# First stage of a three-part block: input and weights by turns on one queue, products among the transposes, angles later

## The reference, cut to what matters

```python
h_res = jnp.concatenate([meta, x], axis=1)
pos = jnp.concatenate([meta_pos, positions + N_META], axis=1)
for l in range(DEPTH):
    h = rmsnorm(h_res, norm_gain[l])
    proj = h @ w_in[l]
    u_pool, z_pool, c_q, c_kv, k_rope, z_mla, g_pool, g_mla = jnp.split(proj, IN_SPLIT_POINTS, axis=-1)
    ...
# in apply_rope
ang = pos.astype(jnp.float32)[..., None] * inv_freq
cos = jnp.cos(ang)[:, :, None, :]
sin = jnp.sin(ang)[:, :, None, :]
```

## Time and profile before

| what | value |
|---|---|
| median of three runs | 1821.43 us (1821.07 to 1821.55) |
| the profiled execution | 1820.53 us, its span 1818.7 us |
| TensorE, VectorE, ScalarE, GpSimd busy | 96%, 65%, 48%, 18% of the span |
| first product of the first layer | starts at 22.25 us |
| c3, the fourth latent chunk | starts at 43.08 us |

### The profile page before, as it was taken

One profiled execution on the slowest core, in us unless ns is written; L12 is line 12 of the kernel. 1 busy time (PEld: TensorE's weight loads), 2 busy tenths in 40 slices (PEclk: granted clock), 3 DMA queues, 4 the chain that ended last, 5 costly groups with the idle time before them and its releaser, 6 DMA issues.

```text
span 1818.7 us, 25325 instructions
## 1 busy us (share of the span) xinstructions
PE 1750.9 (96%) x10156; PEld 1441.4 (79%) x10156; DVE 1185.6 (65%) x1704; ACT 873.7 (48%) x1407; POOL 331.2 (18%) x222
## 2 busy tenths in 40 slices
PE   8999999999999999999999999999999979999993
PEld 7998788999897667788999766765578758888882
DVE  5566645554466655555775698577674467989896
ACT  5425434234334544334344455466552246777771
POOL 3323222001243223001000375300010010000001
PEclk8999999999999999999999999999999989999996
DMA  6203112223312202323222200213152269999994
GB/s 189 76 24 99 47 48 70 94 70 116 96 59 75 70 30 65 100 93 121 76 88 93 70 24 24 70 47 115 50 193 93 93 219 363 402 405 402 405 362 169
DMA packets 156095, 241.31 MB, mean 133 GB/s; under 512 B 9593, under 2 KB 101018, under 8 KB 155978
## 3 DMA queue, kind: packets, MB, share of 16 engines
q1 hardware_dynamic: 148602, 212.88, 33.9%
q0 software_dynamic: 4464, 16.25, 2.4%
q10 hardware_dynamic: 2912, 10.55, 1.4%
HBM read 223.41 MB, written 16.25 MB: 132 GB/s over the span
## 4 chain that ended last, share of the span: by engine, by line
PE 51%; DVE 5%; ACT 4%; issue 2%; DMA 1%; POOL 0%; POOLq 0%; ACTq 0%; DVEq 0%
PE acc L1377 15%; PE acc L876 10%; PE acc L1120 9%; PE acc L1145 7%; PE acc L1209 2%; PE acc L1223 2%; PE acc L1240 1%; PE acc L1363 1%; PE acc L1231 1%; PE acc L1105 1%; DVE upad L2702 1%; DVE qk L2702 1%; ACT v L1973 1%; DMA qk<-y_rows,back_rows 0%; PE acc L1027 0%
## 5 line engine op out<-in xcount | busy, mean ns | idle before, releaser
L876 PE MATMUL acc<-h_split,ring_split 128*128 128x264 f32 (+1 forms) x864 | 269.5, 312 | 0.0
L876 PEld LDWEIGHTS acc<-h_split,ring_split 128*128 128x128 f32 x864 | 162.3, 188 | 9.6
L1145 PE MATMUL acc<-ring_split,h_split 128*128 128x256 f32 x384 | 108.0, 281 | 0.0
L876 PE MATMUL acc<-h_split,qk_split 128*128 128x264 f32 (+1 forms) x288 | 92.7, 322 | 1.3 <-DVE ring_split L2206 1.3
L876 PE MATMUL acc<-ring_split,qk_split 128*128 128x264 f32 (+1 forms) x288 | 92.2, 320 | 0.0
L2206 DVE TENSOR_TENSOR ring_split<-ring,o_split 128x1024 fp32r<-128x1024 f32 (+1 forms) x32 | 44.8, 1417 | 64.2 <-ACT o_split L1535 64.1
L3140 POOL DMA_INDIRECT latent<-h_rows,rows_of x16 | 18.3, 1141 | 355.7 <-PE acc L1363 214.0
L2206 DVE TENSOR_TENSOR ring_split<-ring,qk_split 128x1024 fp32r<-128x1024 f32 (+1 forms) x56 | 59.4, 1069 | 34.0 <-ACT qk_split L1535 34.0
L876 PE MATMUL acc<-h_split,krope_split 128*128 128x264 f32 (+1 forms) x240 | 79.4, 331 | 1.9 <-POOL ring_split L3031 1.9
L3017 POOL TENSOR_TENSOR latent<-latent 128x528 f32<-128x528 f32 x18 | 26.9, 1492 | 293.0 <-ACT latent L1530 292.6
L1377 PE MATMUL acc<-qk_split,krope_split 128*128 128x512 f32 x264 | 78.1, 397 | 0.0
(11 more groups left out here) (596 smaller groups left out, 5536.5 us busy)
## 6 DMA issues: line engine op xcount, KB each, us to landing
ring<-in_w_in SPq DMA_DIRECT2D x64, 1024.0 KB, 5.3
ring<-in_w_expert_gate SPq DMA_DIRECT2D x10, 2048.0 KB, 12.8
ring<-in_w_expert_up SPq DMA_DIRECT2D x10, 2048.0 KB, 12.0
ring<-in_w_expert_down SPq DMA_DIRECT2D x10, 2048.0 KB, 13.4
ring<-in_w_out SPq DMA_DIRECT2D x12, 1024.0 KB, 5.2
y_rows<-gate ACTq DMA_DIRECT2D x16, 512.0 KB, 6.9
hres<-in_w_expert_up SPq DMA_DIRECT2D x3, 2048.0 KB, 11.6
qk<-in_w_expert_down SPq DMA_DIRECT2D x3, 2048.0 KB, 12.9
```

Of the source, the lines that this page charges most:

```text
L876: ins = nc.tensor.matmul(dst[0:rows_, half, 0:x.shape[1]], w[:, k, :], x, start=(k == 0 and i == 0), stop=(k == last and i == 2), skip_gro ...
L1145: ins = nc.tensor.matmul(dst[:, side, 0:WIDE], x[k][:, rows_], w, start=(k == 0 and part == 0), stop=(k == DC - 1 and part == 2), skip_gro ...
```

## The change

x is loaded in two halves of its columns (1 MB each) on SP's queue, by turns with the first two granules of weights; positions, the rest of the constants, the other two granules and all small loads come behind. Only the first layer's first gain, the identity and the meta tokens are loaded by ScalarE. The first gain is turned by itself (`first_gain`), the others later (`vecs`). TensorE runs three fillers at first, turns chunks 0 to 3 with some fillers among them, and turns chunk k + 4 behind step k of `first_products`, in the accumulators of chunks 2 and 3 (`accumulator_again`). VectorE makes the angles in four pieces, each behind the lower weights of one of the entries 3 to 6; ScalarE takes Sin and cos behind c6. The product `ss_h`, the tables and the root stand in the first layer behind c6 instead of c2 (`SUMS_AT`).

```diff
+        SUMS_AT = (6, 2)
...
-            load_first(0, 2)
+            for i in range(2):
+                sp.dma_start(xin[:, :, i * HID:(i + 1) * HID],
+                             a["x"][0, :, i * HID:(i + 1) * HID].rearrange("(j p) d -> p j d", p=P)).then_inc(x_loaded[i], 16)
+                load_first(i, i + 1)
+            sp.dma_start(angles[:, 0, META:T].bitcast(I32),
+                         a["positions"].to_broadcast([ROPE, SEQ])).then_inc(const_loaded, 16)
+            sp.dma_start(const[:, P:], a["const"][:, P:K_TIE]).then_inc(const_loaded, 16)
+            load_first(2, 4)
+            sp.wait_ge(pool_made, at(pool_made, "vrows"))
+            for l in range(LAYERS):
+                load_gains(l)
...
+            def accumulator_again(label, reader, back):
+
+                for x in jobs[-back]:
+                    released(*x)
+                slot = (len(jobs) - back) % ACCS
+                jobs[-back] = [(label, reader, n.layer)]
+                n.slots[label, n.layer] = slot
+                return acc[:, slot, :, :]
...
                         if k == DC - 1:
                             done(ins, ("c", c))
+                    if n.layer == 0 and k < 4:
+                        n.layer = None
+                        turn_input(k + 4)
+                        n.layer = 0
...
+            for c in range(4):
+                turn_input(c)
+                keep_busy(acc[:, 3, 1, 0:256], 1 if c < 2 else 0, work[:, 0, 0:256])
+            keep_busy(acc[:, 3, 1, :], 3, work[:, 0, 0:512])
+
             def turn_tables():
 
+                pe.wait_ge(const_loaded, 32)
+                pe.wait_ge(gains_loaded, at(gains_loaded, "gains"))
+                dst = accumulator("vecs", dve_evacuated)
+                done(nc.tensor.transpose(dst[:, 0, 0:LAYERS * LV], vrows[0:LAYERS * LV, :],
+                                         ident[0:LAYERS * LV, 0:LAYERS * LV]), "vecs")
...
-                    if c == 2:
+                    if c == SUMS_AT[n.layer]:
                         product("ss_h", act_evacuated, [ones[:, :]], lambda k: sum_sq,
                                 before=lambda k: pe.wait_ge(square_sum, at(square_sum, "sum", back=1)))
                         if n.layer == 0:
...
+            act.dma_start(first_gain[0:DC, :], a["norm_gain"][0].rearrange("(k m) -> k m", k=DC))\
+                .then_inc(first_gain_loaded, 16)
+            act.dma_start(const[:, 0:P], a["const"][:, 0:P]).then_inc(ident_loaded, 16)
+            act.dma_start(metain[0:META, :], a["meta_tokens"]).then_inc(meta_loaded, 16)
...
+            input_upper(0)
+            input_copy(2)
+            input_upper(1)
+            first_upper(0)
+            first_upper(1)
+            input_upper(2)
+            input_upper(3)
+            input_copy(5)
+            input_upper(4)
+            first_upper(2)
+            input_upper(5)
+            input_copy(7)
+            input_upper(6)
+            input_upper(7)
             for c in range(DC):
                 squares(c, ("x", c), ("sq0", c))
             for n.layer in range(LAYERS):
...
                     weights_upper(JOBS_A, c + 3)
-                    if c == 2:
+                    if c == SUMS_AT[n.layer]:
+                        if n.layer == 0:
+                            n.layer = None
+                            rotation_tables()
+                            n.layer = 0
                         root("ss_h", inv[:, :], D, 1)
...
+            input_copy(0)
+            input_copy(1)
+            input_lower(0)
+            input_lower(1)
+            first_lower(0)
+            first_lower(1)
+            input_copy(3)
+            input_lower(2)
+            input_lower(3)
+            input_copy(4)
+            input_lower(4)
+            input_copy(6)
+            first_lower(2)
+            for c in range(5, DC):
+                input_lower(c)
...
                 if n.layer == 0:
+                    for i in range(3, DC):
+                        weights_lower(JOBS_A, i)
+                        if i < 7:
+                            n.layer = None
+                            (angles_begun, angles_turns, angles_reduced, angles_ended)[i - 3]()
+                            n.layer = 0
                     n.layer = None
                     turned_tables()
                     n.layer = 0
+                    layer_vectors()
+                    inverse("ss_h", inv[:, :])
```

More of the change, by code:

```diff
@@ L276, in program @@
         vrows2 = qkf[:, 5 * D + P:5 * D + 2 * P]
+        first_gain = qkf[:, 5 * D + 2 * P:5 * D + 3 * P]
+        angles = v[:, :, :].rearrange("p c t -> p (c t)")[NOPE:QK, 0:2 * T].rearrange("p (a t) -> p a t", a=2)
         sum_sq = gate[:, 1, :]
@@ L393, in program @@
         const_loaded = sem("const_loaded")
-        x_loaded = sem("x_loaded")
+        x_loaded = [sem(f"x_loaded{i}") for i in range(2)]
+        meta_loaded = sem("meta_loaded")
+        ident_loaded = sem("ident_loaded")
+        first_gain_loaded = sem("first_gain_loaded")
         vec_loaded = sem("vec_loaded")
@@ L655, in _, with load_gains @@
         def _(sp):
[L656 to L662 removed]
+            def load_gains(l):
                 r = LV * l
@@ L916, in _, with turn_input @@
             done(ins, "meta")
-            for c in range(DC):
-                dst = accumulator(("x", c), act_evacuated if c in X_BY_ACT else dve_evacuated)
+            def turn_input(c):
+                if c % 4 == 0:
+                    pe.wait_ge(x_loaded[c // 4], 16)
+                by = act_evacuated if c in X_BY_ACT else dve_evacuated
+                if c < 4:
+                    dst = accumulator(("x", c), by)
+                else:
+                    dst = accumulator_again(("x", c), by, 4 - c % 2)
                 for i in range(4):
@@ L2184, in _ @@
-            big = 1.5 * 2 ** 23
-            chain(ts(turns, ang, 1.0 / (2 * math.pi), big, ALU.mult, ALU.add))
-            chain(ts(turns, turns, -big, None, ALU.add))
-            rest, parts = 2 * math.pi, []
-            for bits in (8, 12, 24):
-                e = 2.0 ** (bits - 1 - math.floor(math.log2(abs(rest))))
-                parts.append(math.trunc(rest * e) / e if bits < 24 else rest)
-                rest -= parts[-1]
-            for part in parts:
-                chain(stt(out=ang, in0=turns, scalar=-part, in1=ang, op0=ALU.mult, op1=ALU.add))
@@ L2194, in _, with angles_begun @@
[L2194 to L2201 removed]
+            def angles_begun():
+                dve.wait_ge(const_loaded, 32)
+                nc.vector.tensor_copy(ang[:, 0:META], const[NOPE:QK, K_META:K_META + META])
+                chain(nc.vector.tensor_copy(ang[:, META:T], angles[:, 0, META:T].bitcast(I32)))
+                chain(ts(ang[:, META:T], ang[:, META:T], float(META), None, ALU.add))
+                chain(ts(ang, ang, const[NOPE:QK, K_FREQ:K_FREQ + 1], None, ALU.mult))
@@ new lines, in angles_turns, with angles_reduced @@
+            def angles_turns():
+                big = 1.5 * 2 ** 23
+                chain(ts(turns, ang, 1.0 / (2 * math.pi), big, ALU.mult, ALU.add))
+                chain(ts(turns, turns, -big, None, ALU.add))
+            def angles_reduced():
+                rest, parts = 2 * math.pi, []
+                for bits in (8, 12, 24):
+                    e = 2.0 ** (bits - 1 - math.floor(math.log2(abs(rest))))
+                    parts.append(math.trunc(rest * e) / e if bits < 24 else rest)
+                    rest -= parts[-1]
+                for part in parts:
+                    chain(stt(out=ang, in0=turns, scalar=-part, in1=ang, op0=ALU.mult, op1=ALU.add))
@@ new lines, in angles_ended @@
+            def angles_ended():
+                chain(ts(angles[:, 0, :], ang, 3.1415925, -3.1415925, ALU.min, ALU.max))
+                dve.wait_ge(dve_step, now(dve_step))
+                made(stt(out=angles[:, 1, :], in0=angles[:, 0, :], scalar=-1.0,
+                         in1=angles[:, 0, :], op0=ALU.mult, op1=ALU.max), "angles")
+            result("first_gain")
+            slot = n.slot(("first_gain"))
+            evacuated(nc.vector.tensor_copy(vecs[:, 0:DC], acc[:, slot, 0, 0:DC]), "first_gain")
@@ L2285, in _ @@
                     n.layer = 0
-                for i in range(6, DC):
-                    weights_lower(JOBS_A, i)
+                    layer_vectors()
+                    inverse("ss_h", inv[:, :])
+                else:
+                    for i in range(2, 6):
+                        weights_lower(JOBS_A, i)
+                    inverse("ss_h", inv[:, :])
+                    for i in range(6, DC):
+                        weights_lower(JOBS_A, i)
                 def gain_of(x, count):
```

119 lines of the change are left out of this document (52 added, 67 removed).

## The result

The changed kernel takes 1827.62 us (median of seven runs, 1826.96 to 1829.36), the kernel before 1821.19 beside it: ratio 1.0036, 95% interval 1.0026 to 1.0046, so 6.4 us slower. The profiled execution took 1828.59 us, its span 1826.7 (before 1818.7). The busy line of the page says nothing of it: TensorE is busy 1754.5 us, 96% of the span as before.

A forecast was written before the change was run, and what follows sets the result against it. TensorE, busy 96% of the span, was taken to bound the kernel. The terms -5.5 + 6.9 + 3.2 = +4.6 us, added to the median of 1821.43, gave 1826.0 us, range 1820.5 to 1829.5.

The forecast's parts named there:

- Term 1: Start of chunk 3 on TensorE, still waiting for the sum of squares: 37.6 instead of 43.08 us, -5.5 us.
- Term 2: Tables moved behind chunk 6: chunk 7 waits for Sin, cos, two table loads and the root, +6.9 us.
- Rival 3: Between chunks 6 and 7: chunk 7 does not wait for the root, so faster, 1817.5 us; chance 0.06.
- rival 4: Loads at the start: halves and granules share the engines instead of landing by turns, 1829.0 us; chance 0.05.
- rival 5: ScalarE behind chunk 6: a table change holds it twice as long as its load, 1828.6 us; chance 0.03.
- Term 3: TensorE's clock falls to half behind the new waits before chunk 3 and around chunk 6: 1.6 us each, +3.2.
- Rival 1: TensorE's clock stays full through both new waits, before chunk 3 and around chunk 6: 1822.8 us; chance 0.22.
- Rival 2: At the start, the early products run at half clock, squares begin at 24.6 us: 1827.7 us; chance 0.16.
- Sum: Whole forecast shift, read at chunk 7's square: -5.5 + 6.9 + 3.2 = +4.6 us.
- the shift goes through to the end: Behind chunk 7: later stages keep their code, so the +4.6 us there was to reach the kernel's end.

The follow-up runs named there:

- the run with all mends: Changed kernel with small loads first, table load drawn forward, first sum of squares in its own buffer and behind c4, Sin and cos behind c5: 1809.54 us.

## Why the prediction was right, and where its sizes were off

Direction, place and range hold (1826.0 forecast, 1820.5 to 1829.5; 1827.6 measured). That the time came within 1.6 us of the forecast is luck in part: two errors, in term 1 and behind c7, offset each other. By its terms:

- **Term 1**, start of c3: -5.5 us forecast, -1.0 measured (42.08 for 43.08), outside its bounds of -9.2 to -3.0. The mechanism was as described: TensorE idle 4.73 us (5.0 forecast) for a chain of 14.58 us from first square to c3 (14.7 forecast). From the first product to the squares it took 10.0 us (10.1 forecast). What was mis-sized is the stretch ahead of the first product, so that the squares began at 27.50, not 22.9, and even later than the upper bound of 25.35. Two sentences failed. One is "Identity, first gain and meta tokens are 130 KB on the other queue and land before": small and issued early was taken for landing early. Putting them first brings 24.18, 3.3 us. The other is that ScalarE's first table load "now waits for the meta copy, 7.2 to 8.5": it waited for chunk 0's copy, which adds its 1.28 us to the path. With it drawn forward too the squares begin at 23.62, and at 23.10 in the run with all mends, 0.2 us from the forecast; executions of one start differ by more (27.50 to 28.35 in the six kernels that keep the changed start).
- **Term 2**, tables behind c6: +6.9 forecast, and c7 starts 6.69 us after c6's square (6.7 forecast), by the two waits named. Rival 3 (c7 does not wait for the root) is out, rival 4 (halves and granules do not come by turns) too, with x's halves at 5.8 and 12.2 us (6.3 and 12 forecast) and the first weights between them at 9.7, and so is rival 5: the root starts 0.02 us after its table load ends, as before. "0 to 0.3 us" for the lower weights behind the reciprocal was right for this kernel (they are done at 79.3, ahead of c7's end), but only because c7 is late.
- **Term 3**, the clock: +3.2 forecast, +4.4 measured, its upper bound: 1.5 behind c3 (42.08 to 49.72 is 7.64 us, 43.08 to 49.19 before is 6.11) and 2.9 behind c6 (15.58 - 5.80 - 6.9). Rival 1 is out. The row behind 22.25, from which the 1.6 us were taken, is not a clean case: the granted clock was 0.50 from 19 us on, ahead of the wait of 2.77 us.
- **Rival 2**, early products at half clock, did not come true as stated: the first products ran at full clock (1.00 from 17.5 to 19 us). What ran at 0.50 were the turned chunks and fillers ahead of them, from 8.4 to 15.1 us. With the small loads first these ran at 1.00, and from the meta tokens' transposes to the first product it took 8.2 us instead of 9.1, so this cost at most 0.9 us; it is contained in term 1.
- **Sum**: +10.3 at c7 against +4.6. That "the shift goes through to the end" failed as well: at the end of the profiled executions 8.0 us are left (spans of 1826.7 and 1818.7), in the medians 6.4, which brought the time near the forecast. The largest piece lies near 1030 us, in code that the change does not touch. Before:

```profile
1024.64 2.88 DVE L2654 SCALAR_TENSOR_TENSOR gate<-gate,rt 128x512 f32<-128x512 f32 x1
...
1024.61 2.36 POOL L3102 TENSOR_TENSOR ring_split<-ring,o_split 128x1024 fp32r<-128x1024 f32 x1 [152.08 <-ACT o_split L1535]
...
1038.01 0.49 DVE L2653 TENSOR_SCALAR gate<-gate,rt 128x512 f32<-128x512 f32 x1
```

With the change:

```profile
1034.39 0.75 DVE L2776 SCALAR_TENSOR_TENSOR gate<-gate,rt 128x512 f32<-128x512 f32 x1
...
1034.51 2.85 POOL L3224 TENSOR_TENSOR ring_split<-ring,o_split 128x1024 fp32r<-128x1024 f32 x1 [152.05 <-ACT o_split L1580]
...
1044.71 0.56 DVE L2775 TENSOR_SCALAR gate<-gate,rt 128x512 f32<-128x512 f32 x1
```

GpSimd begins 0.03 us before VectorE in the one, 0.12 after it in the other, and VectorE's instruction, for which TensorE waits, takes 2.88 or 0.75 us. From there to the last row, the next turn of the same work, it takes 13.4 us before and 10.3 with the change: 3.1 us of the shift are gone. The two runs made from the kernel before have GpSimd's 2.36 and the long turn as well, the eight made from the changed one 2.84 and the short turn. What shifts the two engines against each other by 0.15 us is open. Later about 1.3 us are lost again, around 1490 us, where the clock is at half for 13.7 us instead of 10.2. The last 1.6 us, between the profiled executions and the medians, are scatter between executions.

## What to carry to other kernels

An earlier start is worth little until the chain behind it is shortened too (here 4.7 us at the first product, 1.0 us at c3): before predicting a gain, follow each buffer that the early work writes to whoever still holds it, and see which slack was just enough. Where several waits lie behind each other, price the ones that are covered: in the kernel before, moving the sum behind c6 cost 6.4 us without Sin, because a reciprocal of 3.45 us stood ready to take its place. Here a pause of 4.7 us cost its length and then 1.5 us of slow clock behind it, and the mends were worth more together (18 us) than the sum of each alone (12.6).

## What the runs showed of the hardware

- Small loads on a second queue are not fast by being small: 64 KB took 5.4 and 6.6 us to land beside 1 MB loads on SP's queue, longer than the first of those (5.1); as SP's first issues they took 1.8 and 2.1 us and are there before TensorE asks for them at 5.93 us. Whether the queue or the order made the difference was not separated.
- VectorE and GpSimd slow each other: an instruction on 32x528 with one tensor as its input takes 1.45 us while GpSimd adds, 0.49 in the kernel before, where GpSimd was idle; three with two tensors take 5.21 instead of 3 x 0.70. The Trainium skill (SBUF — State Buffer, Who interferes with whom) says that the two share a pair of ports, and whichever starts first holds it for the whole instruction; the rows at 1024.6 and 1034.4 us agree, where 0.03 us of lead decide over 2.1 us.
- The same pause of 2.3 us near 580 us (574.6 to 577.0) was followed by half clock in six of the twelve kernels and not in the other six, the one before among the latter; where the two can be set side by side (the small loads first, and the change) it cost 1.6 us. One row of full clock behind a pause is no evidence that pauses of this length are free.
